# Stick-breaking attention: the difference taken on V instead of on the weights

## The reference

```python
z = jnp.einsum('bhqd,bhkd->bhqk', q[:, :, q0:q1], k[:, :, :q1]).astype(jnp.float32) * scale
strict = pos[:q1][None, :] < pos[q0:q1][:, None]
log_keep = jnp.where(strict, jax.nn.log_sigmoid(-z), 0.0)
log_rest = lax.cumsum(log_keep, axis=3, reverse=True) - log_keep
a = jnp.where(strict, jnp.exp(jax.nn.log_sigmoid(z) + log_rest), 0.0)
outs.append(jnp.einsum('bhqk,bhkd->bhqd', a, v[:, :, :q1].astype(jnp.float32)))
```

## Time and profile before

| what | us |
|---|---|
| time, median of 3 runs | 3180.3 (3179.01 to 3183.41) |
| span of the profiled execution, from its first to its last instruction | 3177.3 |
| attention phase of layer 0, kind 0 / 1 / 2 | 38.1 / 39.0 / 45.0 |

### The profile page before, as it was taken

How to read it: one execution, slowest core, us unless ns; L and a number is a source line. 1 busy time by engine, 2 the same in 40 slices (tenths; PEclk the granted TensorE clock), 3 DMA queues, 4 the chain that set the end, 5 groups by cost and what they waited for, 6 DMA issues and landing times.

```text
span 3177.3 us, 36092 instructions
## 1 busy us (share of the span) xinstructions
PE 3005.1 (95%) x14479; PEld 1659.0 (52%) x14479; DVE 1491.1 (47%) x2829; ACT 724.1 (23%) x1521; POOL 355.3 (11%) x218
## 2 busy tenths in 40 slices
PE   8999899998989899999999999999989887999998
PEld 5888443787744344446856533333345543444443
DVE  5994842998392434675575311211144753011112
ACT  1210542121262201111124201100015642111111
POOL 4553000655200000000001100000000000000000
PEclk9999999999999899999999899999999998999999
DMA  5452003456201222110412799999931003999997
GB/s 225 164 194 80 27 1 129 155 184 244 80 1 40 108 83 106 36 53 8 169 67 88 314 389 399 376 389 377 396 122 56 24 3 148 412 421 421 421 421 295
DMA packets 89896, 606.07 MB, mean 191 GB/s; under 512 B 10809, under 2 KB 11612, under 8 KB 19205
## 3 DMA queue, kind: packets, MB, share of 16 engines
q1 hardware_dynamic: 79776, 575.70, 45.4%
q0 software_dynamic: 4432, 15.73, 1.6%
q10 hardware_dynamic: 5524, 12.35, 1.2%
HBM read 592.73 MB, written 11.01 MB: 190 GB/s over the span
## 4 chain that ended last, share of the span: by engine, by line
PE 63%; DVE 7%; ACT 2%; issue 1%; another core or an unknown queue 0%; DVEq 0%; ACTq 0%; PEldq 0%
PE ps L1359 8%; PE ps L2763 7%; PE ps L2725 7%; PE ps L2776 4%; PE ps L2742 4%; PE ps L2806 4%; PE ps L1092 3%; PE ps L3056 2%; PE ps L2613 2%; PE ps L1457 2%; PE ps L2815 2%; PE ps L2529 2%; PE ps L2630 2%; PE ps L1697 2%; PE ps L3217 1%; PE ps L1509 1%
## 5 line engine op out<-in xcount | busy, mean ns | idle before, releaser
L611 PE MATMUL ps<-mem 128*128 128x256 f32 x1792 | 393.3, 381 | 13.2 <-DVE mem L641 10.8
L611 PEld LDWEIGHTS ps<-mem 128*128 128x128 f32 x1792 | 340.3, 191 | 65.5 <-DVE mem L641 14.4
L556 POOL TENSOR_TENSOR mem<-mem 128x512 f32<-128x512 f32 (+1 forms) x160 | 301.7, 1885 | 535.2 <-DVE mem L852 276.5
L754 DVE SCALAR_TENSOR_TENSOR mem<-mem 128x1024 f32<-128x1024 f32 x160 | 254.7, 1632 | 13.8 <-DMA mem<-in_ada_w 12.9
L1359 PE MATMUL ps<-mem 128*128 128x512 f32 (+1 forms) x768 | 254.7, 494 | 2.9 <-ACT mem L1200 2.9
L2763 PE MATMUL ps<-mem 128*64 128x512 f32 x1024 | 223.3, 594 | 0.0
L2725 PE MATMUL ps<-mem 128*64 128x512 f32 x1024 | 222.5, 592 | 0.7 <-ACT mem L2659 0.7
L1359 PEld LDWEIGHTS ps<-mem 128*128 128x128 f32 x768 | 147.5, 193 | 109.5 <-issue 98.3
L641 DVE TENSOR_TENSOR mem<-ps,mem 128x256 f32<-128x256 f32 x308 | 121.3, 418 | 111.9 <-PE ps L611 68.4
L1092 PE MATMUL ps<-mem 128*128 128x512 f32 x384 | 169.6, 597 | 1.8 <-DVEq L156 1.8
L2915 DVE TENSOR_TENSOR mem<-ps,mem 128x512 f32<-128x512 f32 x16 | 11.1, 691 | 314.1 <-PE ps L2725 314.1
(11 more groups left out here) (420 smaller groups left out, 4156.9 us busy)
## 6 DMA issues: line engine op xcount, KB each, us to landing
mem<-in_moe_w SPq DMA_DIRECT2D x384, 1024.0 KB, 13.9
mem<-in_w_in SPq DMA_DIRECT2D x48, 1024.0 KB, 8.1
mem<-in_ada_w SPq DMA_DIRECT2D x48, 1024.0 KB, 5.0
mem<-in_hy_w_in SPq DMA_DIRECT2D x24, 1024.0 KB, 6.9
mem<-in_w_out SPq DMA_DIRECT2D x12, 1024.0 KB, 6.0
mem<-in_k_win_l SPq DMA_DIRECT2D x8, 1024.0 KB, 6.9
mem<-in_hy_w_out SPq DMA_DIRECT2D x8, 1024.0 KB, 5.0
mem<-in_sw_w_in SPq DMA_DIRECT2D x6, 1024.0 KB, 7.1
```

What stands on the lines that cost most here:

```text
L556: gp(out, x, y, op).then_inc(A.mark(sem), 1)
L611: m = mm(seven(l, unit), x[:, k, :], y[:, k, :], start=(k == 0), stop=(k == 3))
L754: stt(PRODUCT if again else w, w, 1.0, C_ROWS[:, z, :], ALU.mult, ALU.mult, accum_out=mod(layer, b // KD, b % KD, z))\
```

## The change

It takes the difference on V instead of on the weights. With V[-1] = 0, the sum over j of (C[j+1] - C[j]) V[j] equals the sum over j of (C[j] - 1) (V[j-1] - V[j]). So:

- V's stick-breaking tiles are replaced, once for each layer, by the row before minus the own row. The row before lies on the neighbouring partition. ScalarE issues two transfers at the start of the attention phase that copy the tiles one partition down into V_BEFORE, which lies in RIGHT's tiles 1 and 2 (127 rows of 8 KB, and one piece of 6 KB for the first partition). GpSimd sets the very first row to zero, waits for both transfers, and subtracts in four instructions of 128x512.
- The subtraction on VectorE (16 for each layer) goes, and so do the four small memsets at the start of the phase. The second scan now releases the transposes.
- The eviction of the stick-breaking transposes is Identity with a bias of -1 from a column of MISC, in place of Copy. VectorE sets this column once, in the first phase.
- The product with V of the first stick-breaking pair (head pair 4 in the list) waits for the four subtractions.
- The new semaphore names are other names for semaphores that are idle in these phases.

```diff
+SHARED_SEMS = {"sums_made": "ctx_full", "v_moved": "ctx_out", "v_stepped": "ctx_turned", "masked": "ctx_silu"}
...
+            for n, other in SHARED_SEMS.items():
+                sems[n] = sems[other]
...
             nc.vector.memset(MISC[:, 2:3], 0.0).then_inc(A.mark(), 1)
+            nc.vector.memset(MISC[:, 3:4], -1.0).then_inc(A.mark(), 1)
...
+        V_BEFORE = v(RIGHT_ + 1024, NQ, 512)
+
+        def act_move_rows(A):
+
+            own = VN[:, NQ:2 * NQ, :]
+            A.e.dma_start(V_BEFORE[1:P], own[0:P - 1]).then_inc(S["v_moved"], 16)
+            A.e.dma_start(V_BEFORE[0:1, 1:NQ, :], own[P - 1:P, 0:NQ - 1, :]).then_inc(S["v_moved"], 16)
+
+        def pool_attn(A):
+
+            A.last, A.counts = None, {}
+            nc.gpsimd.memset(V_BEFORE[0:1, 0, :], 0.0).then_inc(A.mark(), 1)
+            A.e.wait_ge(*A.last)
+            A.e.wait_ge(S["v_moved"], 32)
+            for i in range(NQ):
+                own = VN[:, NQ + i, :]
+                nc.gpsimd.tensor_tensor(own, V_BEFORE[:, i, :], own, ALU.subtract).then_inc(A.mark("v_stepped"), 1)
+            A.last, A.counts = None, {}
...
         def pe_pv(A, hh):
             kind, pair = HEADS[hh]
             A.e.wait_ge(S["turned_out"], NQ * (hh + 1))
+            if (kind, pair) == (1, 0):
+                A.e.wait_ge(S["v_stepped"], NQ)
...
         def act_attn(A):
+            act_move_rows(A)
...
-                    act(dst, src, ACT.Copy).then_inc(A.mark("turned_out"), 1)
+                    if kind == 1:
+                        act(dst, src, ACT.Identity, bias=MISC[:, 3:4]).then_inc(A.mark("turned_out"), 1)
+                    else:
+                        act(dst, src, ACT.Copy).then_inc(A.mark("turned_out"), 1)
...
-            for pset in P_SETS:
-                nc.vector.memset(pset[:, :, 512:513], 1.0).then_inc(A.mark(), 1)
-            A.e.wait_ge(*A.last)
...
                             nc.vector.tensor_tensor_scan(keep, keep, one_col.to_broadcast([P, kw]), 1.0, ALU.mult, ALU.mult)\
-                                .then_inc(A.mark(), 1)
-                        A.e.wait_ge(*A.last)
-                        tt(pset[:, :, 512 - kw:512], pset[:, :, 513 - kw:513], pset[:, :, 512 - kw:512], ALU.subtract)\
-                            .then_inc(A.mark("weights"), 1)
+                                .then_inc(A.mark("weights" if c else None), 1)
...
+                if p in (2, 2 + H_PHASES):
+                    pool_attn(A)
```

More of the change, by code:

```diff
@@ L206, in build @@
                 sems[n] = ctx.enter_context(nc.semaphore(f"{n}_{turn}"))
-            nums = [x.num for x in sems.values()]
+            for n, other in SHARED_SEMS.items():
+                sems[n] = sems[other]
+            nums = sorted({x.num for x in sems.values()})
             assert max(nums) - min(nums) == len(nums) - 1
```

## The result

The changed kernel takes 3228.0 us (3226.4 to 3229.9, four runs) against 3179.7 (3178.6 to 3183.4, four runs): a ratio of 1.0151, 95% interval 1.0139 to 1.0164. The forecast was 3177.5 us, with 3171.5 to 3183.5 as its range. The profiled execution's span is 3225.3 us against 3177.3, 48.0 us more.

The account below looks back on a forecast made before the run. VectorE was taken to set the stick-breaking pace, with TensorE the next limit. Relief -8.0, bias +2.1, GpSimd's turns +3.1 and transfers 0 gave -2.8 us: 3180.3 to 3177.5 us, range 3171.5 to 3183.5.

Parts of the forecast that it names:

- What is moved: the two transfers: Start of attention, ScalarE: 1.41 us of idle covers issuing, so 0, or 0.9 us a layer uncovered; data lands after 8 us.
- The rival of the table loads: Stick-breaking evictions: Identity and Sigmoid in separate tables would force reloads on ScalarE, +47 us, some 3224 us; chance 0.03.
- GpSimd's turns: Kind 0: GpSimd's subtractions and VectorE's SBUF instructions shut each other out; 2.2 us in layer 1, 0.9 in layer 0, sum 3.1.
- the rival of the clock: Start of attention: a shifted low-clock stretch moves the time about 1.9 us either way; chance 0.05 together with the unforeseen.
- The relief: Stick-breaking and the start of forgetting: without VectorE's subtraction TensorE's waits go, 3.5 + 0.5 = 4.0 us a layer, 8.0 for both.
- The bias: Stick-breaking evictions on ScalarE: 0.09 us more each, 12 of 16 delay TensorE, 1.1 us a layer, 2.1 for both.
- my bound of 8.2: Kind 0: each of eight GpSimd instructions costs VectorE a full 1.03 us turn; as a rival 3182.6 us, chance 0.12.
- What follows ... shifts along: Behind the attention: work is not tied to absolute time, so it moves along with the attention's change; no cost counted.

Follow-up runs that it names:

- e4: The kernel before plus only the two transfers on ScalarE, with the first stick-breaking product waiting for them and their data unused: 3220.2 us, ratio 1.0124.
- e9: The changed kernel with its same two transfers issued by SyncE, behind four loads of the output matrix, instead of by ScalarE: 3182.8 us, ratio 1.0008.
- e1: The changed kernel with its two transfers in the other order, the 6 KB piece first and then the 127 rows: 3184.4 us, ratio 1.0013.
- e3: The changed kernel without transfers, GpSimd's subtractions and the wait for them, so V is not differenced; the biased eviction stays: 3172.4 us, ratio 0.9974.
- e5: e3 with a plain Copy eviction in place of the biased Identity, so the -1 is left out too: 3167.8 us, ratio 0.9964.
- e10: Full computation: against the changed kernel, SyncE moves 112 rows, 15 rows and the piece, and VectorE instead of GpSimd does the four subtractions: 3172.4 us, ratio 0.9976.
- e12: e10 with the eviction as Copy and -1.0 as a number in the instruction, instead of Identity with a bias from memory: 3168.8 us, ratio 0.9965.
- e7: The changed kernel without the transfers; GpSimd subtracts whatever lies in V_BEFORE at once as the phase starts: 3180.3 us, ratio 1.0003.
- e2: The changed kernel with the 127 rows moved as two transfers, 112 and 15 rows, then the 6 KB piece: 3188.2 us, ratio 1.0023.
- e6: e2 without GpSimd's memset and subtractions; the first stick-breaking product waits for the three transfers and V stays undifferenced: 3174.7 us, ratio 0.9986.
- e11: e3 with GpSimd clearing one row of 512 columns five times at the start of each attention phase, which no other engine waits for: 3178.6 us, ratio 0.9996.

## Why the prediction was wrong, step by step

**The step that failed is "What is moved: the two transfers".** I costed the issues as 0, from a single issue of 0.33 us, and the landing at 8 us, from loads that fill all 16 engines. Neither row has an access of 127 partitions, nor a second transfer behind a slow one. The runs showed in their place: one engine, GpSimd waiting 45.3 us for the rows, and an issue held for 19.64 and 20.85 us. e4 has only this and costs 39.8 us; e9 has the same transfers with another issuer and ends at +2.6; e1 has them in the other order and ends at +4.0. So the hold on ScalarE is shown to be the cause, and the slow transfer alone is not. I saw that the issues stand ahead of ScalarE's first Exp and that 1.41 us of idle time must cover them, but bounded their price by 0.9 us, from that single issue. No rival held a slower issue, so nothing in the range could reach the result. The rival of the table loads gave 3224 us, near the 3228.0 measured; that is luck, for its mechanism is absent. Both failings have one root: the prices of a DMA were taken by bytes, and not by shape and by what stands ahead in the queue.

**The whole of the 48 us.** From before to after by stretches: kind 0 +22.7 and +25.0, stick-breaking -3.0 twice, forgetting -0.6 twice, between +7.1, the start and the rest +0.3; together 47.9. Kind 0 splits by e3 and e4: the hold 19.4 and 20.3; GpSimd's turns with what goes with the clock 4.8 and 4.7 (after less e4); and in layer 0 -1.5, since that stretch was 38.1 us at a clock of 0.82 before and 36.6 at 0.91 in e3, which has no edit there but the four memsets. That last is the rival of the clock, at about its size of 1.9 us.

**The relief held.** Forecast: 4.0 us in each layer without the bias, 3.5 and 0.5. e5 has 3.9 less in the stick-breaking stretch and 0.6 less in the forgetting one, 4.5 in all. TensorE sets the pace as said, which the period shows after the change; transposes of the widest unit and the evictions beside them:

```profile
399.68 1.09 PE L991 MATMUL ps<-mem 128*128 128x128 f32 x8
...
408.44 1.09 PE L991 MATMUL ps<-mem 128*128 128x128 f32 x8
```

```profile
405.84 0.69 ACT L1029 ACTIVATE mem<-ps,mem 128x512 f32<-128x512 f32 x1 [1.94 <-PE ps L991]
```

The period is 8.76 us; the forecast had 8.9, before 9.83. Neither row of TensorE has an idle time in brackets, where 1.20 us stood twice. In e5, without the bias, the same transposes start at 367.24 and 375.74: a period of 8.50 where the forecast had 8.63. So the relief is 1.33 us a period and not 1.20, and the bias takes back 0.26, as forecast (0.27).

**The bias held**: 2.1 us forecast, 1.8 in the stretches (e3 less e5, e10 less e12). The medians differ by 4.6 and 3.7, the profiled spans by 3.0 and 4.9; of these spans' differences 1.4 and 2.8 us stand in the untouched rest, and why it moves stays open. No table was loaded for Identity: the stick-breaking stretch has the one load of Sigmoid at its start. So the rival of the tables falls.

**GpSimd's turns were mis-sized by their place.** I forecast 3.1 us for both layers, with GpSimd at work 8 to 16 us into the phase. The two kind-0 stretches are 3.8 us longer with GpSimd at work 1 to 6 us into the phase (e7 less e3), 6.1 longer at 12 to 18 us (e2 less e6) and 9.5 longer at 46 to 52 us (after less e4). But not all of that is turns. If the same VectorE instructions of two such traces are laid side by side from the first scores on, VectorE falls behind by 0.9 and 0.9 us in e7, 2.7 and 2.2 in e2, and 3.4 and 3.2 in after, from GpSimd's first subtraction to the first maxima behind its last. So the turns themselves are 1.8, 4.9 and 6.6 us, all within my bound of 8.2. The forecast lies between the first two. The remaining 2.0, 1.2 and 2.9 us arise before or behind GpSimd's work, where the granted clock is lower than in the partner kernel: 0.70 from 370.7 to 380.6 us in after, against 1.00 over the same last 10 us of kind 0 in e4. This split is read from the timelines; no run here tests it apart from the clock. The timeline of after beside GpSimd, and two of the same instructions undisturbed 9 us earlier:

```profile
365.24 5.37 POOL L959 TENSOR_TENSOR mem<-mem 128x512 f32<-128x512 f32 x4 [45.27 <-DMA mem<-mem]
```

```profile
356.51 0.42 DVE L1090 TENSOR_SCALAR mem<-mem 128x384 f32<-128x384 f32 x1
356.96 0.62 DVE L1092 SCALAR_TENSOR_TENSOR mem<-mem 128x384 f32<-128x384 f32 x1
...
365.23 1.49 DVE L1090 TENSOR_SCALAR mem<-mem 128x384 f32<-128x384 f32 x1
366.76 1.50 DVE L1092 SCALAR_TENSOR_TENSOR mem<-mem 128x384 f32<-128x384 f32 x1
...
368.70 0.70 DVE L1088 TENSOR_TENSOR mem<-mem 128x1 f32<-128x1 f32 x1
```

A multiplication of one column (L1088, 0.16 us alone) waits as well, 0.54 us here and 0.95 in e7, so the price does not shrink with the tile. The scaling L1090, a tensor_scalar, pays like the multiply-add L1092 (1.07 and 0.88 us more); before the change no row had one beside GpSimd.

**"What follows ... shifts along" was wrong by 7 us.** The stretch between the attentions is 412.4 to 415.9 us in the seven kernels whose GpSimd has nothing in the attention phase, and 417.1 to 421.3 in the seven where it has. The gap between the two groups is only 1.2 us in these single executions; the medians of e3 and e11, 6.1 us apart, carry the reading more safely. e11 shows that GpSimd's having instructions there is enough, without a transfer, without another engine that waits for it and without a subtraction.

## What to carry to other kernels

Cost a transfer by the shape that it is issued with, and look for a transfer's share of the 16 engines in the trace: a shift by one partition is 127 rows, and that number has no small divisor. Never put a transfer behind another on an engine that computes, unless a row shows the second one's issue; issue it from an engine that has nothing urgent behind it. A saving on the pacing engine is given back where the replacing work runs on a neighbour that takes turns with it: here the idle time of VectorE itself in the relieved stretch was the free place (e10), and a constant belongs into the instruction (e12).

## What I had not expected of the hardware

**A held issue.** A 6 KB transfer's issue takes 0.64 us ahead of the 127 rows (e1), 0.56 behind 112 and 15 rows (e2), and 19.6 to 21.0 behind the 127 rows (after, e4, layer 0 of e9), but 5.74 in layer 1 of e9. That the first transfer's queue on its one engine must drain to some point would fit; what sets the length, and why e9's second is short, stays open.

**A stretch that depends on GpSimd's earlier instructions.** Layer 1's projection, over 100 us behind the first attention, begins alike in e3 and e11, to some 0.03 us, for 20 us. Timeline of GpSimd and the VectorE instruction beside it, e3:

```profile
574.75 2.61 POOL L562 TENSOR_TENSOR mem<-mem 128x512 f32<-128x512 f32 x2 [0.17 <-POOL mem L562]
577.79 4.30 POOL L562 TENSOR_TENSOR mem<-mem 128x512 f32<-128x512 f32 x2 [0.44 <-POOL mem L562]
```

```profile
577.55 1.22 DVE L760 SCALAR_TENSOR_TENSOR mem<-mem 128x1024 f32<-128x1024 f32 x1
```

and e11:

```profile
574.73 6.24 POOL L562 TENSOR_TENSOR mem<-mem 128x512 f32<-128x512 f32 x4 [0.17 <-POOL mem L562]
```

```profile
577.51 2.32 DVE L760 SCALAR_TENSOR_TENSOR mem<-mem 128x1024 f32<-128x1024 f32 x1
```

In e3 GpSimd pauses 0.44 us behind its tenth instruction, VectorE gets in first and takes 1.22 us; in e11 the pause there is 0.14 us, and VectorE's instruction takes 2.32. From there on the two engines alternate in another order, and by the end of the stretch VectorE has been busy 268.5 us instead of 262.1 and TensorE has waited 9.2 instead of 6.0 us for it. The pause stands at this place in all seven kernels without GpSimd instructions in the attention and in none of the seven with them. A second pause, 0.43 us ahead of the 68th instruction of the stretch in all seven without, stands three instructions earlier, at 0.46 us, in six of the seven with them. So this pause moved when five instructions were added ahead of it. What makes the pauses isn't in the records, and that they decide the length of the stretch was not tried.
